# Hybrid decoder layer on one core: u and v rows per slot by a plan, and one ring of ten for both

## What is computed

```
h = x + W_out( concat[ headnorm(A(xn)), subln(B(xn)) ] ),  xn = RMSNorm(x)
y = h + PEER(RMSNorm(h))
  A: causal dilated sliding-window attention (8 heads), B: causal differential attention (4 heads, 2 maps each)

def expert_chunk(args):            # PEER, for a chunk of 128 tokens
    xc, ic, gc = args
    u = u_table[ic]                # ic: (128, 8 heads, 16 picks) of 16384 experts
    act = gelu(einsum('cd,chkd->chk', xc, u)) * gc
    v = v_table[ic]
    return einsum('chk,chkd->cd', act, v)
```

## Time and profile before

| | |
|---|---|
| three runs | 3414.3, 3417.74, 3423.0 us |
| median | 3417.74 us |
| the profiled execution | 3414.01 us |
| its span, first to last instruction | 3412.1 us |
| mean granted clock of PE over the span | 0.844 of 2.4 GHz |
| moved | 1228.7 MB, mean 360 GB/s |
| gathers (queue q0) | 1073.87 MB, 82.9% of 16 DMA engines' span |
| POOL, one gather | mean 1.09 us (u) and 1.12 us (v) x 1024 each |

### The profile page before, as it was taken

One profiled execution on the slowest core, in us unless ns is written; L12 is line 12 of the kernel. 1 busy time (PEld: TensorE's weight loads), 2 busy tenths in 40 slices (PEclk: granted clock), 3 DMA queues, 4 the chain that ended last, 5 costly groups with the idle time before them and its releaser, 6 DMA issues.

```text
span 3412.1 us, 32695 instructions
## 1 busy us (share of the span) xinstructions
PE 2484.3 (73%) x10208; PEld 1240.6 (36%) x10208; DVE 2140.7 (63%) x5638; ACT 841.5 (25%) x2613; POOL 2257.5 (66%) x2052
## 2 busy tenths in 40 slices
PE   7777878767888667765876678765976678765555
PEld 6565444543445422331423223331433234331111
DVE  2278544885548856587557857586657856586441
ACT  4222423333233323111321123111421133111111
POOL 0026765657666667777777777777777777777775
PEclk9788889988999878887888879886987789886778
DMA  8379999999999999999999999999999999999998
GB/s 261 111 265 320 367 349 374 395 343 371 344 386 386 331 365 357 401 396 393 365 374 397 392 373 391 385 397 386 345 378 402 395 368 344 391 375 376 383 383 290
DMA packets 390076, 1228.70 MB, mean 360 GB/s; under 512 B 43152, under 2 KB 84112, under 8 KB 389904
## 3 DMA queue, kind: packets, MB, share of 16 engines
q0 software_dynamic: 294912, 1073.87, 82.9%
q1 hardware_dynamic: 90576, 152.34, 12.4%
q10 hardware_dynamic: 4416, 0.40, 0.1%
HBM read 1214.40 MB, written 12.06 MB: 359 GB/s over the span
## 4 chain that ended last, share of the span: by engine, by line
PE 39%; POOL 21%; issue 18%; DMA 14%; DVE 7%; ACT 2%; SPq 0%; DVEq 0%; POOLq 0%
PE psum L812 19%; POOL big L608 11%; DMA big<-in_peer_v,big 10%; POOL big L597 10%; PE psum L663 7%; PE psum L783 3%; PE psum L705 3%; DVE big L1278 2%; PE psum L759 2%; PE psum L738 2%; DMA big<-in_w_in 1%; PE psum L722 1%; DMA big<-in_peer_u,big 1%; DMA big<-h_scratch 1%; ACT big L908 1%
## 5 line engine op out<-in xcount | busy, mean ns | idle before, releaser
L812 PE MATMUL psum<-big 128*64 128x512 f32 x4096 | 1299.3, 764 | 807.8 <-issue 742.8
L1278 DVE CUSTOM_DVE_ANT_0 big<-big 128x1024 f32<-128x1024 f32 x1024 | 1241.4, 1223 | 597.8 <-DMA big<-in_peer_u,big 590.4
L597 POOL DMA_INDIRECT big<-in_peer_u,big x1024 | 1115.0, 1089 | 663.7 <-issue 288.2
L608 POOL DMA_INDIRECT big<-in_peer_v,big x1024 | 1142.2, 1115 | 480.8 <-issue 257.6
L812 PEld LDWEIGHTS psum<-big 128*64 128x64 f32 x4096 | 328.6, 162 | 1495.0 <-issue 1483.2
L953 ACT ACTIVATE big<-big 128x64 f32<-128x64 f32 x1024 | 295.7, 338 | 953.0 <-PE psum L812 952.8
L783 PEld LDWEIGHTS psum<-big 128*128 128x128 f32 x2048 | 254.7, 202 | 91.0 <-issue 78.9
L783 PE MATMUL psum<-big 128*128 128x128 f32 x2048 | 273.0, 289 | 8.9 <-ACT big L1005 8.9
L1116 DVE CUSTOM_DVE_ANT_0 big<-psum,big 128x128 f32<-128x128 f32 (+7 forms) x128 | 97.0, 758 | 258.1 <-PE psum L705 256.0
L663 PE MATMUL psum<-big 128*128 128x256 f32 x960 | 235.5, 398 | 14.6 <-DMA big<-in_w_in 14.6
L663 PEld LDWEIGHTS psum<-big 128*128 128x128 f32 x960 | 183.1, 197 | 106.5 <-issue 64.5
(11 more groups left out here) (120 smaller groups left out, 1792.1 us busy)
## 6 DMA issues: line engine op xcount, KB each, us to landing
big<-in_w_peer_q SPq DMA_DIRECT2D x128, 512.0 KB, 8.2
big<-in_w_in SPq DMA_DIRECT2D x24, 1024.0 KB, 11.9
big<-in_peer_u,big POOLq DMA_INDIRECT x1024, 6.6
big<-in_peer_v,big POOLq DMA_INDIRECT x1024, 6.5
big<-in_w_out SPq DMA_DIRECT2D x24, 512.0 KB, 5.7
big<-in_w_in SPq DMA_DIRECT2D x48, 256.0 KB, 9.7
V<-in_x SPq DMA_DIRECT2D x8, 512.0 KB, 14.6
big<-in_x SPq DMA_DIRECT2D x8, 512.0 KB, 8.7
```

The costliest lines, as they stand in the source:

```text
L597: nc.gpsimd.indirect_dma_start(out=u_ring[:, g % RU, :], out_offset=None, in_=peer_u, in_offset=bass.IndirectOffsetOnAxis(ap=idx[:, t % 2, ...
L608: nc.gpsimd.indirect_dma_start(out=v_ring[:, g % RV, :], out_offset=None, in_=peer_v, in_offset=bass.IndirectOffsetOnAxis(ap=idx_v[:, t % ...
L812: last = nc.tensor.matmul(pAcc[half_rows(c), n, :], sel[:, (g + c) % RD, :], v_ring[:, (g + c) % RV, n * COLS:(n + 1) * COLS], start=(p == ...
L1278: v.tensor_tensor_reduce(out=row_, in0=row_, in1=hn[:, t % 2, :], scale=1.0, scalar=0.0, op0=ALU.mult, op1=ALU.add, accum_out=dot[:, t % 2 ...
```

## The change

Rows are given to slots by a plan that is worked out when the kernel is built. `plan_rows` walks over slots and asks in each how many rows are due. `paced` is the old pace of two per slot from slot 38 on, less 20 rows over stages 1 to 7. `lead` adds to u, and takes from v, up to 24 e / 7 rows in stage e: it grows over slots 0 to 25 and falls back to zero over slots 26 to 63. v rows still come in pairs, so a slot has one to three u rows and no, one or two pairs of v. Within a slot the gathers of both kinds are interleaved.

```diff
+LEAD_SLOTS = 26
-RU = RV = 5
+RR = 10
-def rows_at(e, s):
-
-    return divmod(max(lin(e, s) + SLOTS - ROWS_AT, 0), SLOTS)
+def lead(e, s):
+
+    if not 0 <= e < TILES:
+        return 0.0
+    return 24 * e / (TILES - 1) * (min((s + 1) / LEAD_SLOTS, (SLOTS - 1 - s) / (SLOTS - LEAD_SLOTS)))
+
+
+def paced(e, s):
+
+    n = lin(e, s) + 1 - ROWS_AT
+    return 2 * n - 20 * min(max(n, 0), (TILES - 1) * SLOTS) / ((TILES - 1) * SLOTS)
+
+
+def plan_rows():
+
+    us, vs, order = {}, {}, []
+    nu = nv = n = 0
+    while nv < SEQ:
+        e, s = divmod(n, SLOTS)
+        due = paced(e, s)
+        us[n] = list(range(nu, max(nu, min(SEQ, int(due + lead(e, s) + 0.5)))))
+        nu += len(us[n])
+        vs[n] = list(range(nv, max(nv, min(SEQ, 2 * int((due - LAG - lead(e, s) + 1.0) / 2))), PAIR))
+        nv += PAIR * len(vs[n])
+        items = [((i + 0.5) / len(us[n]), 0, ("u", g)) for i, g in enumerate(us[n])]
+        items += [((i + 0.75) / len(vs[n]) / PAIR, 1, ("v", g)) for i, g in enumerate(p + c for p in vs[n] for c in range(PAIR))]
+        order += [item for _, _, item in sorted(items)]
+        n += 1
+    return us, vs, order, n
...
-            for g in range(SEQ + LAG):
-                if g < SEQ:
-                    gather_u(g)
-                if g >= LAG:
-                    gather_v(g - LAG)
+            for i, (kind, g) in enumerate(GATHERS):
+                if kind == "u":
+                    gather_u(i, g)
+                else:
+                    gather_v(i, g)
```

More of the change, by code:

```diff
@@ L853, in _ @@
                         if third == 1:
-                            g = v_pick(re, PAIR * r)
-                            if g is not None:
+                            for g in pairs[0:1]:
                                 add_rows(g)
@@ L862, in _ @@
                                 turn_unit(u)
+                    for g in pairs[1:]:
+                        add_rows(g)
                     t = x_at(e, s, 1 if e >= 0 else 0)
@@ L1016, in _ @@
                 for s in slots(stage):
-                    re, r = rows_at(stage, s)
-                    for p in (2 * r + 2, 2 * r + 3):
-                        g = v_pick(re, p)
-                        if g is not None:
-                            make_sel(g)
+                    for g in V_AT.get(lin(stage, s) + 1, []):
+                        for c in range(PAIR):
+                            make_sel(g + c)
                     u = unit_at(stage, s, 1)
@@ L1026, in _ @@
                         front_early(tf, s)
-                    j = (re - 1) * GROUPS + r // 8 - 1
-                    if r % 8 == 0 and 0 <= j < TILES * GROUPS:
+                    for j in group_at(stage, s, 1):
                         gelu(j)
@@ L1316, in _ @@
                         front_a(tf, s)
-                    if r == LAG // 2 and re >= 2:
-                        finish(re - 2)
-                    if tu is not None:
-                        dot_row(tu, 2 * r + 1)
+                    t = tile_at(e, s)
+                    if t is not None:
+                        finish(t)
+                    for g in picks[len(picks) // 2:]:
+                        dot_row(g)
                     if tf is not None:
```

90 lines of the change are left out of this document (50 added, 40 removed).

## The result

| | before | after |
|---|---|---|
| median of 20 runs each | 3421.56 us | 3444.62 us |
| lowest and highest | 3401.87, 3443.67 | 3423.9, 3469.41 |
| ratio, 95% interval | | 1.007 (1.0047 to 1.0092) |
| profiled execution: span | 3412.1 us | 3446.6 us |
| mean granted clock | 0.844 | 0.849 |

The change makes the kernel slower by 0.7%. The forecast of 3387 us has the wrong sign, and its range (to 3422) doesn't hold the time.

What follows compares the result with a forecast made beforehand. The prediction took transfers as the bound. Its terms, -14 us and -5 us beside the attention and -12 us at the end, gave -31 us on the 3412.1 us span, forecast as a 3387 us median, range 3359 to 3422.

Steps and rivals of the forecast that it cites:

- The first step: Whole kernel: transfers bound it, at a DMA share of 0.97 to 1.01 from 374 to 3352 us.
- ceiling of "some 50" us: Whole kernel: the most the change could win, the time in which transfers are not saturated, 49 us.
- More u rows beside the attention: Stage 7's attention: 16 more dots add 18 us to DVE, hidden in its idle time, cost nothing.
- The signs of being wrong: Attention short but selection longer; clock below 0.85; POOL's waits for PE grown in the selection; DVE without idle time.
- Clock of PE: Attention: gaps in PE may lower its granted clock (0.97 in stage 7, 0.83 in stage 3); left out of the sum.
- Rival 2: Beside the attention, PE's clock falls and half of the 19 us is lost: 3397 us; chance 0.08.
- the -14 us: Attention of stages 5 to 7: fewer v rows shorten slots by 14 us, range 6 to 18; stages 3 and 4 nothing.
- gain of 5: Stages 1 and 2: fewer v pairs beside the attention win 1 us and 4 us.
- The end: Last 24 v rows: ten slots let gathers go faster than the 49.5 us before, a gain of 12 us, bounds 4 and 16.
- The ring and the slowdown: Stages: moving 40 rows to the tail costs 0; one ring of ten changes nothing until v rows come alone.
- Rival 3: In the selection, PE becomes the bound and is slower, a loss of 45 us: 3431 us; chance 0.14.
- Rival 1: Attention runs faster, but longer waits in the selection take it back; only the tail gains, 8 us: 3410 us; chance 0.18.

Runs made afterwards that it cites:

- the last two kernels: The changed kernel with half dots, eleven row and three weight buffers: 3314.09 us (0.9708) without lead and slowdown, 3307.03 us (0.9695) with both.
- the ring alone: The changed kernel with lead and slowdown both at zero, keeping one ring of ten buffers for u and v rows: 3469.59 us, 0.9983 of before.
- The run with both reliefs: The change with plain sums in place of dots and pairs of zeros keeping PE busy beside the attention: 3314.8 us, 0.9697 of before.

## Why the prediction was wrong

**The limit.** The first step failed: "So this is a kernel bound by its transfers, and what it can still win is the time in which they are not saturated". The DMA share is no measure of the pace. In the rows shown, 0.92 went with 328 GB/s, 1.00 with 376 to 388, 1.01 with 386 to 399, 1.02 with 404 to 407. The 1.38 us a row of "pure gathers", taken as the transfers' pace, was POOL's: the row read for it has POOL busy 154.39 us with 146 gathers, and with 0.30 us ahead of each that is 198 of 201 us. My own remark, that a starved transfer counts its waiting as busy, was used for one bound only and not for the limit itself. The ceiling of "some 50" us was wrong by it: the last two kernels gain 96 to 103 us with the same rows moved.

**More u rows beside the attention, "Cost nothing, covered by 11 us of idle DVE".** The dots did fit on DVE (94.91 us, 94 forecast). The cost lies on POOL, whose queue I passed with "one wait per gather as before". POOL had 12 us to spare in stage 7 (76 x 1.365 of 116 us), and 16 more dots lengthened its gathers by 75 x 0.17 = 13 us. The row on it was there: gathers of 0.94 us alone and of 1.149 us beside the selection, and that difference was not asked about. The signs of being wrong asked whether DVE would be without idle time; it was not (94.91 of 118 us), and the dots cost all the same, on another engine.

**Clock of PE.** "so my sum leaves the clock out" was the other failure: 0.97 became 0.89 in stage 7, 0.92 became 0.84 in stage 6, 0.93 became 0.85 in stage 5, and two pairs of 3.68 us stood in the attention of stage 7. Rival 2 named this, at 10 us (3397 for 3387). Its half of the gain assumed the transfers as the other limit; nothing of the gain was left, which I put down to POOL standing there.

**The sum's terms.** PE's slots got as short as forecast (4.7 and 6.7 us), yet the -14 us became +9 over stages 3 to 7 (569 to 578 us), and slots 19 to 26 were not in the sum at all. Stages 1 and 2: 867 us became 859 with 10 rows less, which are 14 us, so no gain of 5. The end was right, -12. The ring and the slowdown cost nothing, as forecast (0.9983 and 0.9968, 1.0003). The selection got 24 us shorter over seven stages, but 25 of 64 slots' share of the 55 us is 21, and the slowdown alone, without the lead, took it from 1124 to 1100 us (first group, the ring alone and with the slowdown). So the relieved DVE gave little. Rival 3 fell: PE is 106 of 148 us busy there at a clock of 0.88. Rival 1 didn't happen either: the attention never got faster.

**What is shown and what isn't.** Shown: the loss is the lead's (two pairs of runs on one chip); free gathers alone do not bring it back (0.66% with sums), nor does PE's clock raised by zero pairs; shorter holds together with one buffer more do. That held gathers fill POOL beside the attention is read from the trace of the change. Argued: that POOL and PE's clock are two limits of equal height. The run with both reliefs is 3% faster than the kernel before, but on a chip where rows came faster, and without a partner that has no lead. A rival stands beside it, that uneven slots need more room in the ring: the lead's cost doubled with eight buffers, and was gone in a kernel that also had eleven. Open: how the 0.65% divides between the three; whether half dots or the eleventh buffer frees the lead, since no run had the lead with one of them alone; and why sums gave 1% in one ring of ten and nothing in two rings of five, which were measured in different groups of runs.

## What to carry to other kernels

A DMA share of 1.00 is no proof that transfers are the bound: compare GB/s at that share between stretches, and add up the issuing engine, its busy time and the gap ahead of each transfer, before you call it idle. When work is moved between engines, add up every engine that the moved instruction can hold, the one that issues the transfers too, and not only those that execute it. Where two limits may be equally high, lifting one can show nothing: test them together, in one group of runs and with a partner that lacks only the change, before either is dismissed.

## What the runs showed of the hardware

- A dot of 128 x 1024 with both inputs in SBUF holds a gather's issue until 0.8 us after its own end (0.94 to 1.99 us); the gather doesn't slow the dot. A plain sum of the same row doesn't hold it (0.95 us in the mean). Halves of 512 columns brought the time to 0.9785 (0.9983 with whole dots, on another chip), for 109 us more of DVE's time.
- Gathers of 512 KB were issued 1.24 us apart at best, and then landed 1.28 us apart, at 406 GB/s.
- Row buffers of 512 KB: 8, 10, 11, 12 gave 1.090, 0.998, 0.984, 0.990 of the time before. The 8 ran with the slowdown, the 11 and 12 on another chip and with three and two weight buffers for four.
- 52 matmul groups of zeros (103.9 us on PE) left the ratio at 1.0088, where the change had 1.0070 and 1.0066 in other groups; the clock beside the attention of stage 5 went from 0.85 to 0.90.
